# The third weight block moved ahead of the meeting at the end of a page loop

## What is computed

```python
def project_in(x, ...):
    xn = rmsnorm(x, g_attn_norm)
    z = jnp.einsum('bsd,de->bse', xn, w_in)
    qa, ka, va, oa, ia, fa, cq, ckv, kr, gate_a, gate_b = split_cols(z)
...
def mla_attend(q, k, c_kv, mask, w_uv):
    s = jnp.einsum('bqhe,bkhe->bhqk', q, k) * ATTN_SCALE
    p = jax.nn.softmax(jnp.where(mask, s, -jnp.inf), axis=-1)
    o_lat = jnp.einsum('bhqk,bkc->bqhc', p, c_kv)
    return jnp.einsum('bqhc,chv->bqhv', o_lat, w_uv)
...
def layer(...):
    h_a, C, n, m = mlstm_branch(q_a, k_a, v_a, i_pre, f_pre, o_pre, C0, n0, m0, g_mlstm_out)
    h_b = attend(q_b, c_kv, k_rope)          # samples: mla_sample, over the paged cache
    merged = sigmoid(gate_a) * (h_a @ w_branch_a) + sigmoid(gate_b) * (h_b @ w_branch_b)
```

## Time and profile before

| | |
|---|---|
| median of 3 runs | 2788.78 us (2787.17 to 2791.51) |
| the profiled execution | 2789.54 us, span 2787.7 us |
| TensorE busy | 2749.5 us (99%) |
| VectorE, ScalarE, GpSimd busy | 1627.4, 1290.1, 403.8 us |
| moved by DMA | 393.56 MB, mean 141 GB/s |
| matmuls | 19368 |
| mean granted TensorE clock | 0.997 |

### The profile page before, as it was taken

How to read it: one execution, slowest core, us unless ns; L and a number is a source line. 1 busy time by engine, 2 the same in 40 slices (tenths; PEclk the granted TensorE clock), 3 DMA queues, 4 the chain that set the end, 5 groups by cost and what they waited for, 6 DMA issues and landing times.

```text
span 2787.7 us, 54352 instructions
## 1 busy us (share of the span) xinstructions
PE 2749.5 (99%) x19368; PEld 2621.2 (94%) x19368; DVE 1627.4 (58%) x2717; ACT 1290.1 (46%) x2320; POOL 403.8 (14%) x766
## 2 busy tenths in 40 slices
PE   9998999999999999999999999999999999999999
PEld 9865899999999989999999999999999999999999
DVE  5466866666666654555554344456677644777644
ACT  4536665555556544444443333344444433444433
POOL 0103333343334310000000000022000000000000
PEclk9999999999999999999999999999999999999999
DMA  7524111222122177656657555575555456555464
GB/s 239 198 69 111 36 51 51 64 57 54 48 63 63 38 235 206 188 173 189 183 174 208 164 165 164 165 196 164 166 166 166 142 164 189 162 160 166 144 185 124
DMA packets 714806, 393.56 MB, mean 141 GB/s; under 512 B 84552, under 2 KB 696594, under 8 KB 714008
## 3 DMA queue, kind: packets, MB, share of 16 engines
q1 hardware_dynamic: 702292, 378.61, 47.0%
q10 hardware_dynamic: 11940, 11.53, 1.2%
q0 software_dynamic: 368, 0.81, 0.1%
HBM read 370.49 MB, written 22.75 MB: 141 GB/s over the span
## 4 chain that ended last, share of the span: by engine, by line
PE 60%; DVE 1%; issue 1%; ACT 1%; ACTq 0%; DVEq 0%
PE bank L302 19%; PE bank L303 19%; PE bank L307 19%; PE bank L2747 0%; ACT sqm L2811 0%; PE bank L2725 0%; PE bank L2735 0%; DVE hn L2910 0%; PE bank L3265 0%; PE bank L2732 0%; PE bank L3308 0%; PE bank L2721 0%; DVE hn L2905 0%; ACT dws L2805 0%; DVE ns L2892 0%
## 5 line engine op out<-in xcount | busy, mean ns | idle before, releaser
L290 DVE TENSOR_TENSOR w_lo_b<-stage,w_hi_b 128x2048 fp32r<-128x2048 f32 (+2 forms) x286 | 612.2, 2141 | 404.6 <-ACT w_hi_b L283 400.7
L283 ACT ACTIVATE w_hi_b<-stage 128x2048 fp32r<-128x2048 f32 (+1 forms) x284 | 508.3, 1790 | 560.8 <-PE bank L307 525.5
L302 PE MATMUL bank<-xnH,w_hi_b 128*128 128x288 f32 (+1 forms) x2736 | 742.9, 299 | 2.5 <-PEq L191 2.5
L303 PE MATMUL bank<-xnL,w_hi_b 128*128 128x288 f32 (+1 forms) x2736 | 737.8, 296 | 0.0
L302 PEld LDWEIGHTS bank<-xnH,w_hi_b 128*128 128x128 f32 (+1 forms) x2736 | 515.0, 188 | 12.0 <-issue 11.4
L303 PEld LDWEIGHTS bank<-xnL,w_hi_b 128*128 128x128 f32 (+1 forms) x2736 | 514.6, 188 | 0.3
L1741 PE MATMUL bank<-uk_all,lat 128*128 128x384 f32 (+1 forms) x1344 | 444.6, 331 | 16.7 <-DVE lat L2536 6.0
L1743 PE MATMUL bank<-uk_all,lat 128*128 128x384 f32 (+1 forms) x1344 | 435.0, 324 | 0.0
L307 PE MATMUL bank<-xnH,w_lo_b 128*128 128x288 f32 (+1 forms) x2736 | 389.6, 295 | 0.0
L307 PEld LDWEIGHTS bank<-xnH,w_lo_b 128*128 128x128 f32 (+1 forms) x2736 | 371.6, 188 | 0.0
L1741 PEld LDWEIGHTS bank<-uk_all,lat 128*128 128x128 f32 x1344 | 253.6, 189 | 33.6 <-issue 22.9
(11 more groups left out here) (541 smaller groups left out, 3756.4 us busy)
## 6 DMA issues: line engine op xcount, KB each, us to landing
stage<-in_w_in_dram SPq DMA_DIRECT2D x88, 1024.0 KB, 5.3
stage<-in_w_up_dram SPq DMA_DIRECT2D x88, 1024.0 KB, 5.4
stage<-in_w_down_dram SPq DMA_DIRECT2D x64, 704.0 KB, 4.5
raw<-in_cache_kv_latent_dram SPq DMA_DIRECT2D x256, 64.0 KB, 1.8
stage<-in_w_branch_a_dram SPq DMA_DIRECT2D x16, 1024.0 KB, 5.5
stage<-in_w_branch_b_dram SPq DMA_DIRECT2D x16, 1024.0 KB, 5.4
stage<-in_w_out_dram SPq DMA_DIRECT2D x16, 1024.0 KB, 5.9
vals<-in_cache_kv_latent_dram SPq DMA_DIRECT2D x60, 256.0 KB, 2.9
```

Source lines behind the costliest of these rows:

```text
L283: act.activation(h, a, ACT.Copy).then_inc(w_hi, 1)
L290: dve.tensor_tensor(lo, a, h.bitcast(F32), ALU.subtract).then_inc(w_lo, 1)
L302: pe.matmul(out, hi, xH(k), start=first and k == 0, stop=False)
L303: pe.matmul(out, hi, xL(k), start=False, stop=False)
```

## The change

- TensorE takes block N0 + 2 in front of the meeting: the first five pieces of its high part between the turnings and the value-up products, the other eleven between these and the transposes, its low part behind the transposes. The transposes use banks 0 and 6 instead of 0 and 3, since block N0 + 2 is in bank 3.
- ScalarE rounds N0 + 3 too in front of the meeting, VectorE makes the low part of N0 + 2 there. Behind the meeting all three skip one block more.
- SyncE asks for N0 before the value rows of the last sample, and for N0 + 2 before the value-up loads.
- ScalarE rounds its half of N0 in two quarters; TensorE waits for the second before piece 4 (f_wq), VectorE before its low part.

```diff
--- before.py
+++ after.py
@@ -1583,9 +1583,9 @@
             dum = sb(ph, "dum", [P, 1])
             c_rows = cb[:].rearrange("p n w -> p (n w)")[0:N_S, 0:KVL]
             g_in, g_pe, g_act, g_cp, g_a, g_z, g_m, g_f = (sem("g_" + x) for x in ("in", "pe", "act", "cp", "a", "z", "m", "f"))
-            f_uv, f_hq, f_hq2, f_wh = sem("f_uv"), sem("f_hq"), sem("f_hq2"), sem("f_wh")
+            f_uv, f_hq, f_hq2, f_wh, f_wq = sem("f_uv"), sem("f_hq"), sem("f_hq2"), sem("f_wh"), sem("f_wq")
             first_raw, first_hi = stage[:, N0 % 4, :], ws["hi"][:, N0 % 2, :]
-            first_half, second_half = slice(0, KC * P // 2), slice(KC * P // 2, KC * P)
+            first_quarter, second_quarter, second_half = slice(0, KC * P // 4), slice(KC * P // 4, KC * P // 2), slice(KC * P // 2, KC * P)
             q_tmp, q_add, q_hi, q_part = (sem("qs_" + x) for x in ("tmp", "add", "hi", "part"))
             uk_hi, uk_lo = (sem("uk_" + x) for x in ("hi", "lo"))
             f_t, f_sum4, a_hi, a_lo, f_rh, f_rl, f_ss = (sem("p_" + x) for x in ("t", "sum", "hi", "lo", "rh", "rl", "ss"))
@@ -1712,17 +1712,17 @@
                     reload(xnL, xnL_dram, 10, 15)
                     for j in range(4, NPG):
                         last_rows(b, j)
-                    for j in range(4):
-                        value_rows(b, j)
                     sp.wait_ge(k_p[4], upto(b, NG - 2))
                     head_load(sp, At(0), 0)
                     sp.wait_ge(k_p[4], upto(b, NG - 1))
                     reload(xnL, xnL_dram, 15, 16, xn_last)
                     head_load(sp, At(0), 1)
                     for j in range(4):
+                        value_rows(b, j)
+                    head_load(sp, At(0), 2)
+                    for j in range(4):
                         uv_load(j)
-                    for m in range(2, 4):
-                        head_load(sp, At(0), m)
+                    head_load(sp, At(0), 3)
                     sp.wait_ge(f_hev, 2)
                     sp.dma_start(hbs_dram, hs).then_inc(e_st[0], 16)
 
@@ -1913,10 +1913,13 @@
                     p3(b, NG - 1)
                     p4(b, NG - 1)
 
-                    def block_high(n):
-                        pe.wait_ge(w_hi, n + 1)
-                        pe.wait_ge(z_free[n % 4], n // 4)
-                        for k in range(KC):
+                    def block_high(n, k0=0, k1=KC):
+                        if k0 == 0:
+                            pe.wait_ge(w_hi, n + 1)
+                            pe.wait_ge(z_free[n % 4], n // 4)
+                        for k in range(k0, k1):
+                            if n == N0 and k == KC // 4:
+                                pe.wait_ge(f_wq, 1)
                             if n == N0 and k == KC // 2:
                                 pe.wait_ge(f_wh, 1)
                             if n == N0 and k == KC - 1:
@@ -1945,6 +1948,7 @@
                     pe.matmul(bank[5][HQ:, 0:1], psums[:, b.mod(2), :], ones[:, 0:1], start=True, stop=True).then_inc(f_sum, 1)
                     block_low(N0 + 1)
                     turn_out(b)
+                    block_high(N0 + 2, 0, 5)
                     pe.wait_ge(e_sc, pairs(b, PR - 1))
                     pe.wait_ge(uv_in, 16 * LC)
                     pe.wait_ge(f_oev, NB)
@@ -1954,11 +1958,13 @@
                                 mm = pe.matmul(bank[(4, 7)[j // 2]][g * N_S:(g + 1) * N_S, j % 2 * P:(j % 2 + 1) * P], olat[:, k, 4 * j + g, :],
                                                uv_of(j)[:, k, g * BV:(g + 1) * BV], start=k == 0, stop=k == LC - 1)
                         mm.then_inc(f_uv, 1)
+                    block_high(N0 + 2, 5, KC)
                     for i, ready in enumerate((f_hq, f_hq2)):
                         pe.wait_ge(ready, 1)
                         for j in range(2):
-                            tr = pe.transpose(bank[3 * i][:, j * P:(j + 1) * P], ol[:, (2 * i + j) * P:(2 * i + j + 1) * P], ident)
+                            tr = pe.transpose(bank[6 * i][:, j * P:(j + 1) * P], ol[:, (2 * i + j) * P:(2 * i + j + 1) * P], ident)
                         tr.then_inc(f_h, 1)
+                    block_low(N0 + 2)
 
                 @blk.scalar
                 def _(act):
@@ -2152,18 +2158,20 @@
                     act.wait_ge(k_p[4], upto(b, NG - 1))
                     act.wait_ge(w_landed[N0 % 4], 16 * (N0 // 4 + 1))
                     act.wait_ge(w_done, N0 - 1)
-                    act.activation(first_hi[:, first_half], first_raw[:, first_half], ACT.Copy).then_inc(w_hi, 1)
+                    act.activation(first_hi[:, first_quarter], first_raw[:, first_quarter], ACT.Copy).then_inc(w_hi, 1)
+                    act.activation(first_hi[:, second_quarter], first_raw[:, second_quarter], ACT.Copy).then_inc(f_wq, 1)
                     square(b, NG - 1, C21, e_c21, e_q21)
                     root(b)
                     act.activation(dum[:], eps, ACT.Exp)
                     split_hi(act, At(N0 + 1))
                     exps(b)
                     split_hi(act, At(N0 + 2))
+                    split_hi(act, At(N0 + 3))
                     act.wait_ge(f_uv, 4)
                     act.activation(ol[:, 2 * P:], bank[7][:, 0:2 * P], ACT.Copy).then_inc(f_hq2, 1)
                     for i in range(2):
                         act.wait_ge(f_h, i + 1)
-                        act.activation(hs[:, 8 * i:8 * i + 8, :].rearrange("p h s -> p (h s)"), bank[3 * i][:, 0:2 * P], ACT.Copy).then_inc(f_hev, 1)
+                        act.activation(hs[:, 8 * i:8 * i + 8, :].rearrange("p h s -> p (h s)"), bank[6 * i][:, 0:2 * P], ACT.Copy).then_inc(f_hev, 1)
 
                 @blk.gpsimd
                 def _(pool):
@@ -2576,6 +2584,7 @@
                     norm_sum(b, NG - 1, C21, 1, 0, e_q21, e_r21)
                     scale_a(b)
                     dve.wait_ge(f_wh, 1)
+                    dve.wait_ge(f_wq, 1)
                     split_lo(dve, At(N0))
                     out_turned(b - 1)
                     scale_b(b)
@@ -2587,6 +2596,7 @@
                     inverse(b, 5)
                     out(b)
                     out_turned(b)
+                    split_lo(dve, At(N0 + 2))
                     dve.wait_ge(f_uv, 2)
                     dve.tensor_copy(ol[:, 0:2 * P], bank[4][:, 0:2 * P]).then_inc(f_hq, 1)
         kept.close()
@@ -2753,7 +2763,7 @@
                             pe.wait_ge(H["ncp"], AH)
                             pe.wait_ge(H["nall"], AH)
                             pe.transpose(bank[4][0:AH + NB * AH, 0:P], n_all[:], ident).then_inc(H["t"], 1)
-                        if blocks and not (h.i is None and h.c == 0 and j < 2):
+                        if blocks and not (h.i is None and h.c == 0 and j < 3):
                             block(pe, n + j, n + j, lambda k: xnH[:, k, :], lambda k: xnL[:, k, :])
                         if chain and j < 6:
                             step(h - 1, j)
@@ -2828,7 +2838,7 @@
                 def heads_(h, n, blocks, chain):
                     for j in range(steps(h)):
                         if blocks:
-                            if not (h.i is None and h.c == 0 and j < 2):
+                            if not (h.i is None and h.c == 0 and j < 3):
                                 split_hi(act, n + (j + 1))
                             if h.i is None and h.c == AH:
                                 act.wait_ge(w_done, N_A + j + 1)
@@ -2934,7 +2944,7 @@
                 def heads_(h, n, blocks, chain):
                     for j in range(steps(h)):
                         if blocks:
-                            if not (h.i is None and h.c == 0 and j < 1):
+                            if not (h.i is None and h.c == 0 and j < 2):
                                 split_lo(dve, n + (j + 1))
                         if h.i is None and h.c == AH and j == GATES - 2:
                             dve.wait_ge(H["t"], 3 * AH + 1)
```

## The result

| | before | changed |
|---|---|---|
| median | 2790.15 us (2786.46 to 2791.84, 6 runs) | 2797.03 us (2794.57 to 2801.55, 6 runs) |
| profiled execution, its span | 2789.54, 2787.7 us | 2797.76, 2795.9 us |
| ratio of the times | | 1.0022, 95% interval 1.0012 to 1.0033 |

The change costs 0.22%, about 6.1 us by the ratio (the two medians are 6.9 apart). Forecast were 4.6 us and 2793.4, with a range to 2797.9. Three more runs of the kernel before had moved its own median up by 1.4 us, to 2790.15; over 33 later runs it was 2791.52. The forecast of the difference was better than that of the time.

What follows compares the result with a forecast made beforehand. TensorE, busy 99% of the span, bounds the kernel; +2.2 us stall ahead of N0+4 and +2.4 low clock behind it give +4.6, 2794.1 against the profiled execution, 2793.4 for the median, range 2788.4 to 2797.9.

Steps and rivals of the forecast that it cites:

- The stall: Ahead of N0+4: its load moves with the meeting, N0+3 alone covers it, TensorE waits 4.7 to 6.4 us; +2.2 us.
- The clock after the stall: Behind the wait ahead of N0+4: the granted clock falls again, price between 1.65 and 4.2, taken as 2.4 us.
- Rival 2: Behind the stall: clock stays low for 8.4 us, price 4.2, so +6.4 in all, 2795.2 us; chance 0.15.
- The start of N0: Block N0: load issued 0.15 us sooner and first quarter rounded 0.43 sooner, so TensorE starts 0.6 us sooner.
- rival 1: Start of N0: the clock doesn't fall there, saving 1.65 us, about 1.2 usable, 2792.2 us; chance 0.20.
- with 1 us to spare: Ahead of the value-up products: their last load lands by 1040.0, needed at 1041.0, so the reordered loads are covered.
- rival 4: Value-up loads late by another 2 us, as if each MB took 3.0: 1 us hole before the meeting, 2794.4; chance 0.07.
- 2.7 us for each MB of value-up, 3.9 for that block: SyncE queue ahead of the meeting: landing times per value-up MB and for N0+2, one after the other.
- the end of the meeting: Meeting of all engines: TensorE is now last and resumes at 1052.03, so it ends 3.78 us later for every engine.
- no change: Total time within 0.2%, 5.6 us, of before: chance 0.78, on its slow side; slower by more 0.19.

Runs made afterwards that it cites:

- the early load without the third block: Kernel before, with SyncE asking for N0+4 in front of the meeting and N0+2 still behind it: 2790.97 us, ratio 1.0000.
- the first edits: Alone on the kernel before: N0 asked for ahead of the value rows, now behind N0+1, its first half rounded in quarters; 2790.56 us, ratio 0.9997.

## Why the prediction was right, and where it wasn't

**The stall.** The step on which the forecast stood came out as it was worked: N0+4 was to start at 1064.82, which is 52.99 from the point; it started at 53.00. The +2.2 us is +2.21. The mechanism is shown; that the number is met to 0.01 us is luck. TensorE resumed 0.16 later than worked out and the load took 0.1 longer, while 0.05 us passed between the rounding and the first matmul, not 0.25; and two larger errors ahead of the meeting cancelled, as told below. The wait is 6.01 us, in the range of 4.7 to 6.4, its long end because the clock was up at N0+3. Both ways of taking the wait away, an earlier issue and an emptier queue, give the time back; the early load without the third block gives nothing.

**The clock after the stall.** Priced at 2.4 between 1.65 and 4.2; from the start of N0+4 to the reading of its result the difference grows from 2.21 to 4.52, so 2.31. A half-rate stretch of 5.1 us fits it. The Trainium skill's rule ("TensorE: Matmul & The Clock Gate", "HAM oscillation — how this bites in real kernels"), that a group of matmuls behind a wait for data starts cold, holds for this wait: the clock is 0.50 from 1068.1 on. Behind shorter waits it did not always (the last section). Rival 2 (8.4 us of low clock) did not come.

**Two steps on the way were wrong and cancelled.** The start of N0 was to gain 0.6 us and gained 0.94: the issue came as early as said, but the rounding began 5.15 us behind it instead of 5.47. More came from the clock, which stayed up at N0. That was rival 1, with a chance of 0.20; it happened in all eight profiles with the first edits. Of the 1.65 us of the clock, rival 1 counted 1.2 as usable; 0.6 came, since TensorE then waited 0.72 for the maxima. The turnings began 1.55 us sooner instead of 0.6. Then the value-up loads, "with 1 us to spare", were late: rival 4, chance 0.07. TensorE came 0.9 us sooner than worked out (28.29 from the point where 29.19 was forecast), and the last load landed at 1044.4, which is 29.2, where 28.2 was forecast. The landings of N0+2, issued at 1025.96, and of the last value-up load, issued at 1031.76:

```profile
stage<-in_w_in_dram SPq DMA_DIRECT2D x1, 1024.0 KB, 7.2
...
uv_lat<-in_w_uv_dram SPq DMA_DIRECT2D x1, 1024.0 KB, 12.6
```

The step that failed is "2.7 us for each MB of value-up, 3.9 for that block", added up over 6 MB without an error of its own. The value rows landed at 13.4 from the point (forecast 13.5). Block N0+2 behind them took 4.7 us instead of 3.9 (landed at 18.0 instead of 17.4), the four value-up loads 11.2 instead of 10.8. In the four other profiles with this order the four took 12.0 to 12.2 us, which is 3.0 for each and the price that rival 4 named. The whole margin was 1 us. I should have seen that rivals 1 and 4 belong together, since the sooner TensorE arrives, the later the loads are for it. The two errors, 0.95 us gained and 1.08 lost, nearly cancel, which is luck: they left the end of the meeting at +3.94 where +3.78 was forecast.

**The absolute time.** 2797.03 is 3.6 above the point forecast. Some 0.5 to 2.7 of that is the median of the three runs of before, 2788.78, which was low for this kernel: 2790.15 with three more, 2791.52 and 2791.42 over 33 each in two later series, 2789.31 over 15 in the last. A median of three from a kernel whose runs spread over 8 us carries about that error, and the range should name it as a term by itself.

**The chances.** The change lies at the edge of what I had called no change (0.2%), on the slow side, where 0.78 and 0.19 met. The sign was forecast by the mechanism, and the mechanism's runs bear it out.

## What to carry to other kernels

When work is moved to the front of a meeting of all engines, everything issued behind the meeting moves back with it. Ask for each load issued there how long it takes to land and what is left to cover it; here a block of 6.4 us was taken out of a cover that had 1.8 to spare. If the buffer is free, move the load's issue with the work, or at least ahead of other large loads in the same queue: a few lines for either made the change worth 0.12% instead of costing 0.22%.

When several loads share a queue, a reordering is a trade between their users. Write down for each load the landing and the first use, and find slots where the queue is idle (as the value rows did), rather than moving the longest wait to another engine's row.

## What of the hardware was not expected

- Around the earlier meeting, between 268 and 310 us, the same code had its clock low for 10.2 us in three of the twelve profiles, for 17 in one and for 20.5 in eight. The point behind it lies between 1011.8 and 1015.6 us: 0.1% of the total time without any cause in the kernels. The length of the low clock is only a part of it: the point is at 1013.4 in one profile with 20.5 us and at 1013.6 in one with 10.2.
- A hole decides less sharply about the clock than I had assumed. Holes of 1.1 to 1.4 us ahead of N0 never brought it down (eight profiles), one of 2.69 did not either, those of 1.92, 2.15 and 3.21 did. Behind the meeting, holes of 2.52 or 2.53 us brought it down in three profiles and not in a fourth, holes of 1.6 to 1.7 never.
- A load of 1 MB of weights, 512 bytes from each row, landed 5.0 to 5.2 us after its issue with nothing ahead of it (N0 in the eight kernels with the first edits), 5.4 to 6.7 right behind the last value rows (N0 in the four without), and 9.7 to 10.5 behind the 1.14 MB of nmb and Cs.
